# Two buffers of one-hots made a step ahead, a choice paced by piece length, and 79 halves in scoring

## Chip, cores and metric

The kernel runs on one core of one Trainium2 chip. The metric is the device time of one execution in microseconds (us), lower is better. Engines are named as in the profile: PE is TensorE, DVE is VectorE, ACT is ScalarE, POOL is GpSimd, SP the engine that only issues transfers.

## What is computed

One layer over 256 tokens of width 2048, all in float32: a normalised input goes through a projection to 5 x 1024 columns, half of them through differential attention and half through a gMLP; then an output projection and a residual; then PEER, an expert layer with 128 x 128 experts; then a final norm. The PEER layer fills most of the time:

```
q = (xb @ w_q).reshape(T, PEER_HEADS, 2, PEER_HALF)
sc = jnp.einsum('thcd,hckd->thck', q, sub_keys)
s1, i1 = lax.top_k(sc[:, :, 0], PEER_TOPK)
s2, i2 = lax.top_k(sc[:, :, 1], PEER_TOPK)
cand = (s1[..., :, None] + s2[..., None, :]).reshape(T, PEER_HEADS, PEER_TOPK * PEER_TOPK)
best, ci = lax.top_k(cand, PEER_TOPK)
...
idx = e1 * PEER_N_KEYS + e2
g = jax.nn.softmax(best.astype(jnp.float32), axis=-1)
act = jax.nn.gelu(jnp.einsum('td,thkd->thk', xb, u_sel))
out = jnp.einsum('thk,thkd->td', g.astype(act.dtype) * act, v_sel)
```

Each token takes 8 heads x 16 = 128 of the 16384 experts.

## The kernel before

**Two ways for two sets of tokens.** For 200 of the 256 tokens (`ND`) the kernel does not gather: it multiplies them with the whole table of `u` (the scoring), applies gelu and a dense matrix of gates that is zero for the experts not taken, and multiplies with the whole table of `v`. For the other 56 tokens it gathers rows of the tables by indirect DMAs of POOL (`gather`), half a row (1024 elements) for each of 128 picks at a time, and DVE makes their dot products and weighted sums: the *halves*, 232 in all (`half_rows`, line 1245 or 1253), each about 1.2 us of DVE. `HALF_STEPS` says in which steps of the scoring one is done, `HALF_UNITS` in which units of the v products. A half waits for its gather; three buffers (`PICKED`) are in turn, and the gather of half k+3 waits for half k.

**Units and steps.** A table comes in units of 128 x 1024 (512 KB, queued by SP). Every unit is split into a high part (ACT, `top`, line 720) and a low part (DVE, `low`, line 1188; POOL in a few steps, `by_pool`, line 477). PE does eight products with the high part and the hi and lo of x side by side (400 columns, line 1634), and one unit later eight with the low part (200 columns, line 1640). A *step* j of the scoring is two units, 2j and 2j+1, and fills row j of `store`. There are 128 steps, then 256 units of v (lines 1674 and 1679).

**What each engine does in a step, in this order.** DVE: `sum_halves(j)` (line 1197: adds the two halves of the PSUM bank, one of them copied out by ACT as `HOLES`, line 745), the low parts of units 2j+4 and 2j+5, then whatever stands in this step beside them, then `land(j)` (line 1224) and the halves. ACT: `HOLES` of step j, the high parts of 2j+5 and 2j+6, the gelu, and what stands beside. PE is one to two steps ahead of DVE's number: the low part made in DVE's step j is multiplied in PE's step j+2.

**Beside the steps** stand, one after another: 

- the *choice* (`piece`, 58 pieces that are left after 24 early ones): top-16 of the scores and of the 256 candidates, then comparisons that turn places into expert numbers. `piece_steps` says how many pieces each step has; before, one in odd and two in even steps, from step 1 to 39. When the pieces of a step are plain (top-16 only), POOL makes one of its two low parts. Two steps after the last piece of each tile of tokens PE transposes the picks (`PICKS_AT`).
- the *spread* of the gates, 50 steps from `SPREAD0` (43 before), four tokens a step: DVE compares indices with 0..127 (`one_hots`, line 1206, into `ONE`), ACT scales one of the two by the gate (`gates_into`, line 766, four instructions), PE multiplies them into a 128 x 128 matrix of gates for each token (`spread`, line 1618, after PE's step), DVE multiplies the rows of `store` that are done (`apply_gates`, line 1216), and ACT copies the gates of the rows to come (`put_gates`, line 757). `ONE` is one buffer, so `one_hots(b)` waits for `spread(b-1)`.
- after the spread, more halves: three in two steps up to step 120.

Before the scoring the queries are made from 32 units, whose low parts DVE and POOL share (`QUERY_BESIDE`, line 464). Early in it POOL also multiplies the 56 gathered tokens by a gain (line 458). The second group of these tokens (`X8`, five loads of 24 rows of 8 KB) was loaded by POOL when the scoring ended.

Of the kernel before, what the change touches and what calls it, by code (L numbers as in the profile page):

```python
# [11 lines left out]
ACT = mybir.ActivationFunctionType  # L12
# [63 lines left out]
QUERY_BESIDE = range(WQ0 + 9, WQ_END, 2)  # L76
CHOICE0 = 1


def piece_steps():  # L80

    steps, j = [], CHOICE0
    rest = 2 * (PIECES - EARLY)
    while len(steps) < rest:
        steps += [j] * min(2 - j % 2, rest - len(steps))
        j += 1
    return [-1] * EARLY + steps[:PIECES - EARLY] + [-1] * EARLY + steps[PIECES - EARLY:]
# [5 lines left out]
              for j in range(NKEYS)}  # L93
# [6 lines left out]
SPREAD0 = PICKS_AT[1] + 2  # L100
# [6 lines left out]
                    + list(range(SPREAD_END, NKEYS - 7, 2)))  # L107
# [14 lines left out]

SEL_A_AT = 2 * NKEYS - 4
# [26 lines left out]
def hybrid_peer_block(nc, x, w_in, w_out, wq_t, keys_t, u_t, peer_u, peer_v, ws_t, bs_t, gain_t, ffn_gain, z_gain,  # L150
                      final_gain, lambdas, rope, out):
    ctx = ExitStack()
    with ctx:  # L153
# [68 lines left out]
        ONE = at("ONE", 108 * KB, [P, 2, TOKB, NKEYS])  # L222
# [180 lines left out]
        def _(pool):  # L403
# [57 lines left out]
            for n in QUERY_BESIDE:  # L461
                pool.wait_ge(hi_ready, n + 1)
                pool.wait_ge(used, n - (LO_SLOTS - 1))
                nc.gpsimd.tensor_tensor(LO[:, n % 2, :], RAW[:, n % 4, :], HI[:, n % 4, :].bitcast(FP32),
                                        ALU.subtract).then_inc(lo_ready[n % 2], 1)
                if n == WQ0 + 9:
                    keys(2)
                if n == WQ0 + 17:
                    keys(3)
                if n - WQ0 in (21, 23, 25, 27):  # L470
                    r = (n - WQ0 - 21) // 2
                    pool.wait_ge(xg_saved, 16)
                    pool.dma_start(X4[r * NA:(r + 1) * NA, :], xg_dram[0:NA, :]).then_inc(x4_ready, 16)
# [41 lines left out]
            for r in range(ROWS_B):  # L515
                pool.dma_start(X8[r * NB_:(r + 1) * NB_, :], xg_dram[NA:NS, :]).then_inc(x8_ready, 16)
# [4 lines left out]
            for k in range(len(HALF_STEPS) + ROW_SLOTS, HALVES):  # L521
                gather(k)
                if HALF_UNITS[k - ROW_SLOTS - len(HALF_STEPS)] >= NKEYS + 50 and late:
                    pool.wait_ge(low_used, N_U + NKEYS + 44)
                    dst, src, done = late.pop(0)
                    pool.dma_start(dst, src).then_inc(done, 16)
# [8 lines left out]
        def _(act):  # L535
# [225 lines left out]
            def gates_into(b):  # L761

                act.wait_ge(compared, b + 1)
                for i in range(TOKB):
                    t = b * TOKB + i
                    ins = nc.scalar.activation(ONE[:, 1, i, :], ONE[:, 1, i, :], ACT.Copy, scale=EG[:, 2, t:t + 1])  # L766
                ins.then_inc(ones, 1)
# [18 lines left out]
            for j in range(NKEYS):  # L786
# [11 lines left out]
                if 0 <= j + 1 - SPREAD0 < N_BATCH:  # L798
                    gates_into(j + 1 - SPREAD0)
# [4 lines left out]
                if j in PICKS_AT:  # L804
                    picks_to_rows(PICKS_AT.index(j))
                if j == FIRST_WEIGHTS_AT:
                    weights_hi(0)
# [44 lines left out]
        def _(dve):  # L852
# [347 lines left out]
            def one_hots(b):  # L1200
# [3 lines left out]
                dve.wait_ge(g_done, b)  # L1204
                t0 = b * TOKB
                v.tensor_tensor(ONE[:], IOTA[:].unsqueeze(1).unsqueeze(1).broadcast_to([P, 2, TOKB, NKEYS]),  # L1206
# [63 lines left out]
            for j in range(NKEYS):  # L1270
# [11 lines left out]
                if 0 <= b + 1 < N_BATCH:  # L1282
                    assert done == [PIECES, PIECES]
                    one_hots(b + 1)
                if 0 <= b < N_BATCH:
                    apply_gates(b)
                if b >= 0:
                    land(j)
# [69 lines left out]
        def _(pe):  # L1358
# [253 lines left out]
            def spread(b):  # L1612
# [4 lines left out]
                for t in range(TOKB):  # L1617
                    last = mm(PS[:, G_BANK + b % 2, t * NKEYS:(t + 1) * NKEYS], ONE[:, 0, t, :], ONE[:, 1, t, :],
# [164 lines left out]
```

## Time and profile before

| | |
|---|---|
| three runs | 1829.03 us median (1823.68 to 1829.89) |
| profiled execution | 1811.19 us, span 1809.4 us, 28831 instructions |
| TensorE clock granted | 0.994 of full over the span |
| PE busy | 1731.2 us, 96% |
| DVE, ACT, POOL busy | 1439.8, 983.7, 478.0 us |
| DMA | 483.79 MB, 267 GB/s in the mean |

The profiled execution is 1% shorter than the three runs. PE's busy time is near the span; what is left is read stage by stage from windows and from the timeline. An idle time in brackets names what ended it.

### The profile page before, as it was taken

The page shows a single profiled execution, that of the slowest core. Times are in us where ns is not written, and L with a number is a line of the kernel's source. Part 1 is how long each engine was busy: PE and PEld are TensorE (multiplying, and loading weights), DVE is VectorE, ACT ScalarE, POOL GpSimd, SP SyncE. Part 2 cuts the span into 40 slices and gives each one's busy share as a digit, 9 for nine tenths or more (in the row PEclk, how much of TensorE's full clock was granted, in tenths as well). Part 3 has the DMA queues.
Part 4 walks back from the last instruction along what each step waited for, and adds up shares of the span by engine and source line. Part 5 has one row for each costly group of instructions (what it writes and reads, how often), then busy time and mean ns, then how long its engine had stood idle before and what let it go on. Part 6 is the DMA issues. An engine that isn't in the chain of part 4 may idle for free. (4 is left out here: it accounts for less than half of the span.)

```text
span 1809.4 us, 28831 instructions
## 1 busy us (share of the span) xinstructions
PE 1731.2 (96%) x10934; PEld 1638.0 (91%) x10934; DVE 1439.8 (80%) x2020; ACT 983.7 (54%) x1600; POOL 478.0 (26%) x327
## 2 busy tenths in 40 slices
PE   8999999999999999889889999999999999999997
PEld 7887788788999999888888999999999999999997
DVE  4546786568799987777788888778889999888995
ACT  5445564443565556666666545555555555555553
POOL 0002300034222001221221445315444224343231
PEclk9999999999999999999999999999999999999998
DMA  7665455666677776666666999899999999999992
GB/s 235 211 186 163 144 159 175 208 223 205 205 225 227 238 242 219 219 221 213 221 215 215 332 348 357 295 309 344 360 348 365 372 358 350 373 377 401 367 375 97
DMA packets 132855, 483.79 MB, mean 267 GB/s; under 512 B 15368, under 2 KB 15522, under 8 KB 132048
## 3 DMA queue, kind: packets, MB, share of 16 engines
q1 hardware_dynamic: 95760, 347.65, 57.4%
q0 software_dynamic: 36672, 133.77, 19.6%
q8 instruction: 87, 1.43, 0.3%
q10 hardware_dynamic: 288, 0.55, 0.1%
q14 instruction: 48, 0.39, 0.1%
HBM read 476.71 MB, written 5.20 MB: 266 GB/s over the span
## 5 line engine op out<-in xcount | busy, mean ns | idle before, releaser
L1674 PE MATMUL PS<-W,HI 128*128 128x400 f32 x2048 | 425.0, 348 | 9.3 <-DVE W L1264 5.6
L1634 PE MATMUL PS<-xT,HI 128*128 128x400 f32 x2048 | 422.2, 348 | 1.6 <-ACT HI L720 1.6
L720 ACT ACTIVATE HI<-V_RAW 128x1024 fp32r<-128x1024 f32 x256 | 271.4, 1061 | 280.0 <-PE PS L1674 135.0
L1674 PEld LDWEIGHTS PS<-W,HI 128*128 128x128 f32 x2048 | 358.4, 189 | 12.7 <-ACT HI L720 6.9
L1634 PEld LDWEIGHTS PS<-xT,HI 128*128 128x128 f32 x2048 | 358.0, 190 | 1.9 <-ACT HI L720 1.7
L1181 DVE TENSOR_TENSOR V_LO<-V_RAW,HI 128x2048 fp32r<-128x2048 f32 x128 | 292.7, 2287 | 24.1 <-ACT HI L720 23.7
L486 POOL DMA_INDIRECT PICKED<-peer_u,PK x116 | 179.5, 1547 | 490.9 <-DVE DOTS L1245 480.8
L720 ACT ACTIVATE HI<-RING_RAW 128x1024 fp32r<-128x1024 f32 x256 | 268.9, 1050 | 46.0 <-DMA RING_RAW<-u_t 41.3
L1188 DVE TENSOR_TENSOR RING_LO<-RING_RAW,HI 128x1024 fp32r<-128x1024 f32 x246 | 289.5, 1217 | 1.6 <-ACT HI L720 1.6
L1640 PEld LDWEIGHTS PS<-xT,RING_LO 128*128 128x128 f32 x2048 | 265.2, 191 | 16.1 <-DVE RING_LO L1188 15.9
L1640 PE MATMUL PS<-xT,RING_LO 128*128 128x200 f32 x2048 | 267.2, 273 | 12.3 <-DVE RING_LO L1188 12.2
L1679 PEld LDWEIGHTS PS<-W,V_LO 128*128 128x128 f32 x2048 | 268.6, 191 | 0.9 <-DVE V_LO L1181 0.9
L1679 PE MATMUL PS<-W,V_LO 128*128 128x200 f32 x2048 | 267.8, 272 | 0.6 <-DVE V_LO L1181 0.6
L486 POOL DMA_INDIRECT PICKED<-peer_v,PK x116 | 178.2, 1537 | 273.5 <-DVE ACC L1253 248.1
L864 DVE TENSOR_TENSOR LO<-RAW,HI 128x1024 fp32r<-128x1024 f32 x120 | 147.7, 1233 | 126.7 <-PE PS L1386 96.1
L538 ACT ACTIVATE HI<-RAW 128x1024 fp32r<-128x1024 f32 x144 | 152.6, 1066 | 163.7 <-PE PS L1386 58.2
L1253 DVE SCALAR_TENSOR_TENSOR ACC<-PICKED,DOTS,ACC 128x1024 f32<-128x1024 f32 (+1 forms) x112 | 142.8, 1281 | 42.4 <-DMA PICKED<-peer_v,PK 41.8
L1245 DVE CUSTOM_DVE_ANT_0 PICKED<-PICKED,X 128x1024 f32<-128x1024 f32 (+1 forms) x116 | 140.7, 1220 | 17.9 <-DMA PICKED<-peer_u,PK 17.7
L1379 PE MATMUL PS<-HI,xT 128*128 128x512 f32 x440 | 139.5, 398 | 2.1 <-ACT xT L563 1.4
L1386 PE MATMUL PS<-HI,xT 128*128 128x512 f32 x440 | 136.1, 391 | 0.6 <-DVE xT L883 0.6
L766 ACT ACTIVATE ONE<-ONE,EG 128x128 f32<-128x128 f32 x200 | 63.9, 390 | 95.6 <-DVE ONE L1206 95.6
L1386 PEld LDWEIGHTS PS<-HI,xT 128*128 128x128 f32 x440 | 82.6, 188 | 18.4 <-DVE xT L883 1.0
(213 smaller groups left out, 1668.0 us busy)
## 6 DMA issues: line engine op xcount, KB each, us to landing
RING_RAW<-u_t SPq DMA_DIRECT2D x256, 512.0 KB, 4.5
V_RAW<-peer_v SPq DMA_DIRECT2D x256, 512.0 KB, 7.3
RAW<-w_in SPq DMA_DIRECT2D x80, 512.0 KB, 3.9
RAW<-w_out SPq DMA_DIRECT2D x32, 512.0 KB, 3.7
RAW<-wq_t SPq DMA_DIRECT2D x32, 512.0 KB, 4.7
x_spill<-X POOLq DMA_DIRECT2D x2, 1024.0 KB, 5.8
X1R<-x_spill POOLq DMA_DIRECT2D x8, 256.0 KB, 10.5
PICKED<-peer_u,PK POOLq DMA_INDIRECT x116, 7.8
```

The costliest lines, as they stand in the source:

```text
L486: pool.indirect_dma_start(PICKED[k % ROW_SLOTS][:], None, table.rearrange("e (a c) -> (e a) c", a=2), bass.IndirectOffsetOnAxis(PK4[:, hal ...
L538: nc.scalar.activation(HI[:, slot, :], RAW[:, slot, :], ACT.Copy).then_inc(hi_ready, 1)
L720: nc.scalar.activation(HI[:, n % HI_SLOTS, :], raw_of(n), ACT.Copy).then_inc(top_ready, 1)
L864: v.tensor_tensor(LO[:, u % 2, :], RAW[:, u % 4, :], HI[:, u % 4, :].bitcast(FP32), ALU.subtract).then_inc(lo_ready[u % 2], 1)
L1181: nc.vector.tensor_tensor(pair_of(V_LO, v), pair_of(V_RAW, v), HI[:, slot:slot + 2, :].bitcast(FP32), ALU.subtract)\
L1188: v.tensor_tensor(low_of(n), raw_of(n), HI[:, n % HI_SLOTS, :].bitcast(FP32), ALU.subtract).then_inc(low_dve, 1)
L1253: ins = v.scalar_tensor_tensor(acc, rows, DOTS[0:np_, 0, g:g + 1], acc, ALU.mult, ALU.add)
L1386: ins = mm(banks[c], low(tt), h[:, halves[c]], start=False, stop=last and tt > 0)
L1634: return mm(PS[:, j % S_BANKS, 0:2 * ND].rearrange("p (a t) -> p a t", a=2), HI[:, n % HI_SLOTS, kk * P:(kk + 1) * P], xT[:, k, :, 0:ND], ...
L1640: return mm(PS[:, j % S_BANKS, 0:ND], low_of(n)[:, kk * P:(kk + 1) * P], xT[:, k, 0, 0:ND], start=False, stop=k == KT - 1)
L1674: return mm(PS[:, V_BANKS[i], 0:2 * ND].rearrange("p (a t) -> p a t", a=2), HI[:, v % HI_SLOTS, i * P:(i + 1) * P], weights_of(v), start=v ...
L1679: return mm(PS[:, V_BANKS[i], 0:ND], low_of(N_U + v)[:, i * P:(i + 1) * P], weights_of(v)[:, 0, :], start=False, stop=v % NKEYS == NKEYS - 1)
```

## The change

It has five parts.

- `ONE` has two buffers. DVE makes `one_hots(b+2)` in the step in which it applies gates b, after the apply instead of before it (before: `one_hots(b+1)`, ahead of the apply), and waits for one product less. ACT scales them one step earlier too, after `put_gates` instead of before.
- `piece_steps` gives pieces by a length for each kind, 2.6 us (3.4 where the piece is plain) of room a step. The 58 pieces take steps 1 to 32 instead of 1 to 39; the spread runs from step 37 to 86 instead of 43 to 92. POOL makes 8 low parts instead of 10.
- After the spread every fourth step has a second half instead of every second one; since this part starts six steps sooner, 79 halves instead of 78 are in the scoring.
- In the query stage DVE makes the low part of unit `WQ0 + 9` instead of POOL, and the keys that POOL loaded after it go with unit `WQ0 + 11`.
- `X8` is loaded after gather 99, about unit 35 of the v products, instead of at the end of the scoring.

```diff
-QUERY_BESIDE = range(WQ0 + 9, WQ_END, 2)
+QUERY_BESIDE = range(WQ0 + 11, WQ_END, 2)
...
+def piece_cost(i):
+
+    if i < HC:
+        return 1.55
+    if HC + 2 <= i < HC + 2 + PH:
+        return 2.35
+    return 0.5 if i in (HC + 2 + PH, HC + 2 + PH + 7) else 1.4
...
-    rest = 2 * (PIECES - EARLY)
-    while len(steps) < rest:
-        steps += [j] * min(2 - j % 2, rest - len(steps))
+    left = [i for o in range(2) for i in range(EARLY, PIECES)]
+    while left:
+        room += 2.6
+        if left[0] in PLAIN and (len(left) < 2 or left[1] in PLAIN):
+            room += 0.8
+        while left and piece_cost(left[0]) <= room + 0.4:
+            room -= piece_cost(left.pop(0))
+            steps.append(j)
         j += 1
...
-SPREAD0 = PICKS_AT[1] + 2
+SPREAD0 = PICKS_AT[1] + 3
...
-                    + list(range(SPREAD_END, NKEYS - 7, 2)))
+                    + list(range(SPREAD_END, NKEYS - 7, 4)))
...
+X8_AT = len(HALF_STEPS) + 20
...
-        ONE = at("ONE", 108 * KB, [P, 2, TOKB, NKEYS])
+        ONE = at("ONE", 104 * KB, [P, 2, 2, TOKB, NKEYS])
...
-            for r in range(ROWS_B):
-                pool.dma_start(X8[r * NB_:(r + 1) * NB_, :], xg_dram[NA:NS, :]).then_inc(x8_ready, 16)
...
+                if k == X8_AT:
+                    for r in range(ROWS_B):
+                        pool.dma_start(X8[r * NB_:(r + 1) * NB_, :], xg_dram[NA:NS, :]).then_inc(x8_ready, 16)
...
-                if 0 <= j + 1 - SPREAD0 < N_BATCH:
-                    gates_into(j + 1 - SPREAD0)
                 if 0 <= j - SPREAD0 < N_BATCH:
                     put_gates(j - SPREAD0)
...
+                if 0 <= j + 2 - SPREAD0 < N_BATCH:
+                    gates_into(j + 2 - SPREAD0)
...
-                dve.wait_ge(g_done, b)
+                if b > 1:
+                    dve.wait_ge(g_done, b - 1)
...
-                if 0 <= b + 1 < N_BATCH:
-                    assert done == [PIECES, PIECES]
-                    one_hots(b + 1)
                 if 0 <= b < N_BATCH:
                     apply_gates(b)
+                if 0 <= b + 2 < N_BATCH:
+                    assert done == [PIECES, PIECES]
+                    one_hots(b + 2)
```

The order on DVE in a step of the spread that also has a half. `TMP<-PS,HOLES` is `sum_halves`, `RING_LO` the two low parts, `ONE` the one-hots, `store<-store,PS` the gates applied, `store<-store,TMP` is `land`, `ISA` the half. Before, step 62:

```order
L1197 TENSOR_TENSOR TMP<-PS,HOLES 128x200 [waits landed,copied,low_used]
L1188 TENSOR_TENSOR RING_LO<-RING_RAW,HI 128x1024 [waits top_ready] x2
L1206 TENSOR_TENSOR ONE<-IOTA,EG 128x1024 [waits g_done]
L1216 TENSOR_TENSOR store<-store,PS 128x62x4 [waits gelus,g_done]
L1224 TENSOR_TENSOR store<-store,TMP 128x80 [waits g_put,gelus]
L1245 ISA PICKED_100,DOTS<-PICKED_100,X_95 128x1024 [waits row_ready0]
```

With the change, the same step (its line numbers are about 17 higher):

```order
L1214 TENSOR_TENSOR TMP<-PS,HOLES 128x200 [waits landed,copied,low_used]
L1205 TENSOR_TENSOR RING_LO<-RING_RAW,HI 128x1024 [waits top_ready] x2
L1234 TENSOR_TENSOR store<-store,PS 128x62x4 [waits gelus,g_done]
L1224 TENSOR_TENSOR ONE<-IOTA,EG 128x1024 [waits g_done]
L1242 TENSOR_TENSOR store<-store,TMP 128x104 [waits g_put,gelus]
L1263 ISA PICKED_101,DOTS<-PICKED_101,X_95 128x1024 [waits row_ready1]
```

The gates are applied ahead of the one-hots, and these are the ones for the product after the next.

The order on ACT in a step of the spread, from one `HOLES` to the next. Before:

```order
L745 ACTIVATE HOLES<-PS 128x8x25 [waits summed,low_used]
L720 ACTIVATE HI<-RING_RAW 128x1024 [waits low_dve,top_used,ring_ready1]
L730 ACTIVATE store<-TMP 128x136 [waits summed]
L731 ACTIVATE TMP<-TMP 128x64
L720 ACTIVATE HI<-RING_RAW 128x1024 [waits low_dve,top_used,ring_ready2]
L766 ACTIVATE ONE<-ONE,EG 128x128 [waits compared]
L766 ACTIVATE ONE<-ONE,EG 128x128 x3
L757 ACTIVATE store<-PS 128x70x4 [waits g_mul]
L745 ACTIVATE HOLES<-PS 128x8x25 [waits summed,low_used]
```

With the change:

```order
L762 ACTIVATE HOLES<-PS 128x8x25 [waits summed,low_used]
L737 ACTIVATE HI<-RING_RAW 128x1024 [waits low_dve,top_used,ring_ready3]
L747 ACTIVATE store<-TMP 128x108 [waits summed]
L748 ACTIVATE TMP<-TMP 128x92
L737 ACTIVATE HI<-RING_RAW 128x1024 [waits low_dve,top_used,ring_ready4]
L774 ACTIVATE store<-PS 128x69x4 [waits g_mul]
L783 ACTIVATE ONE<-ONE,EG 128x128 [waits compared]
L783 ACTIVATE ONE<-ONE,EG 128x128 x3
L762 ACTIVATE HOLES<-PS 128x8x25 [waits summed,low_used]
```

The copy of the gates now stands ahead of the scaling, and between the scaling and the next `HOLES` nothing is left.

## Rows read from the trace of the kernel before

**Rows 1.** The page, busy time of each engine.

```profile
PE 1731.2 (96%) x10934; PEld 1638.0 (91%) x10934; DVE 1439.8 (80%) x2020; ACT 983.7 (54%) x1600; POOL 478.0 (26%) x327
```

**Rows 2.** Windows: choice, spread, steps after it; us, busy by engine, PEclk, DMA share, GB/s.

```profile
469.00:675.60 206.60, 203.34 (x1385) 202.16 (x1384) 188.30 (x365) 120.03 (x181) 35.24 (x25) 1.00 0.71 229
675.60:997.30 321.70, 290.98 (x2002) 282.56 (x2002) 252.37 (x365) 204.19 (x499) 64.05 (x33) 1.00 0.66 219
997.30:1166.80 169.50, 158.88 (x1059) 155.96 (x1058) 146.52 (x210) 85.49 (x136) 73.60 (x44) 0.99 0.93 339
```

**Rows 3.** Timeline of PE at stage bounds: start, us, engine, line, operation.

```profile
656.47 1.64 PE L1634 MATMUL PS<-xT,HI 128*128 128x400 f32 x8
...
675.55 1.64 PE L1634 MATMUL PS<-xT,HI 128*128 128x400 f32 x8
...
997.27 1.64 PE L1634 MATMUL PS<-xT,HI 128*128 128x400 f32 x8
...
1162.09 1.63 PE L1634 MATMUL PS<-xT,HI 128*128 128x400 f32 x8
```

**Rows 4.** Timeline of PE in one step of the spread.

```profile
774.47 1.16 PE L1618 MATMUL PS<-ONE 128*128 128x128 f32 x8 [0.91 <-ACT ONE L766]
...
776.92 1.04 PE L1640 MATMUL PS<-xT,RING_LO 128*128 128x200 f32 x8
777.79 1.64 PE L1634 MATMUL PS<-xT,HI 128*128 128x400 f32 x8
779.27 1.03 PE L1640 MATMUL PS<-xT,RING_LO 128*128 128x200 f32 x8
```

**Rows 5.** Timeline of DVE and ACT around the same step.

```profile
771.89 1.22 DVE L1206 TENSOR_TENSOR ONE<-IOTA,EG 128x1024 f32<-128x1024 f32 x1
773.03 0.38 DVE L1216 TENSOR_TENSOR store<-store,PS 128x228 f32<-128x228 f32 x1
773.14 1.28 ACT L766 ACTIVATE ONE<-ONE,EG 128x128 f32<-128x128 f32 x4 [1.98 <-DVE ONE L1206]
...
774.61 0.33 ACT L745 ACTIVATE HOLES<-PS 128x200 f32<-128x200 f32 x1
774.81 0.22 DVE L1224 TENSOR_TENSOR store<-store,TMP 128x60 f32<-128x60 f32 x1 [1.40 <-ACT store L757]
...
775.16 0.37 DVE L1197 TENSOR_TENSOR TMP<-PS,HOLES 128x200 f32<-128x200 f32 x1
...
777.72 1.22 DVE L1206 TENSOR_TENSOR ONE<-IOTA,EG 128x1024 f32<-128x1024 f32 x1
```

**Rows 6.** Choice: timeline, and DVE's L1197 group in steps 1 to 39.

```profile
474.35 0.37 DVE L1197 TENSOR_TENSOR store<-PS,HOLES 128x200 f32<-128x200 f32 x1 [2.06 <-ACT HOLES L745]
...
615.47 1.14 PE L1640 MATMUL PS<-xT,RING_LO 128*128 128x200 f32 x8 [2.34 <-DVE RING_LO L1188]
...
661.81 0.37 DVE L1197 TENSOR_TENSOR store<-PS,HOLES 128x200 f32<-128x200 f32 x1 [0.91 <-ACT HOLES L745]
...
L1197 DVE TENSOR_TENSOR store<-PS,HOLES 128x200 f32<-128x200 f32 x39 | 14.3, 367 | 9.5 <-ACT HOLES L745 8.4
```

**Rows 7.** DMA issues after the spread: count, KB, median us to landing.

```profile
PICKED<-peer_u,PK POOLq DMA_INDIRECT x26, 8.5
```

**Rows 8.** Timeline of the query stage, units WQ0+8 to WQ0+10.

```profile
384.26 4.77 POOL L458 TENSOR_TENSOR X<-X,FGAIN 56x1024 f32<-56x1024 f32 x2 [4.78 <-DMA X<-xs_spill]
386.33 1.12 PE L1415 MATMUL PS<-xT,LO 128*128 128x256 f32 x8
387.79 2.33 DVE L864 TENSOR_TENSOR LO<-RAW,HI 128x1024 fp32r<-128x1024 f32 x1 [0.35 <-PE PS L1405]
392.38 2.08 PE L1415 MATMUL PS<-xT,LO 128*128 128x256 f32 x8 [3.08 <-POOL LO L464]
```

**Rows 9.** Timeline where the v products begin.

```profile
1171.93 2.59 POOL L516 DMA_DIRECT2D X<-xg_spill  x5 [21.04 <-DVE TMP L1197]
...
1188.09 2.24 ACT L720 ACTIVATE HI<-V_RAW 128x1024 fp32r<-128x1024 f32 x2 [4.72 <-DMA V_RAW<-peer_v]
```

More of the change, by code:

```diff
@@ L75 @@
 EARLY = 12
-QUERY_BESIDE = range(WQ0 + 9, WQ_END, 2)
+QUERY_BESIDE = range(WQ0 + 11, WQ_END, 2)
 CHOICE0 = 1
-def piece_steps():
-    steps, j = [], CHOICE0
-    rest = 2 * (PIECES - EARLY)
-    while len(steps) < rest:
-        steps += [j] * min(2 - j % 2, rest - len(steps))
+def piece_cost(i):
[4 more added lines that the diff above has]
+    return 0.5 if i in (HC + 2 + PH, HC + 2 + PH + 7) else 1.4
+def piece_steps():
+    steps, j, room = [], CHOICE0, 0.0
+    left = [i for o in range(2) for i in range(EARLY, PIECES)]
[6 more added lines that the diff above has]
+            steps.append(j)
         j += 1
-    return [-1] * EARLY + steps[:PIECES - EARLY] + [-1] * EARLY + steps[PIECES - EARLY:]
+    n = PIECES - EARLY
+    return [-1] * EARLY + steps[:n] + [-1] * EARLY + steps[n:]
 PIECE_STEPS = piece_steps()
@@ L465, in _ @@
                                         ALU.subtract).then_inc(lo_ready[n % 2], 1)
-                if n == WQ0 + 9:
+                if n == WQ0 + 11:
                     keys(2)
@@ L765, in gates_into @@
                     t = b * TOKB + i
-                    ins = nc.scalar.activation(ONE[:, 1, i, :], ONE[:, 1, i, :], ACT.Copy, scale=EG[:, 2, t:t + 1])
+                    ins = nc.scalar.activation(ONE[:, b % 2, 1, i, :], ONE[:, b % 2, 1, i, :], ACT.Copy, scale=EG[:, 2, t:t + 1])
                 ins.then_inc(ones, 1)
@@ L1203, in one_hots @@
                     dve.wait_ge(picks_out, TT)
-                dve.wait_ge(g_done, b)
+                if b > 1:
+                    dve.wait_ge(g_done, b - 1)
                 t0 = b * TOKB
-                v.tensor_tensor(ONE[:], IOTA[:].unsqueeze(1).unsqueeze(1).broadcast_to([P, 2, TOKB, NKEYS]),
+                v.tensor_tensor(ONE[:, b % 2], IOTA[:].unsqueeze(1).unsqueeze(1).broadcast_to([P, 2, TOKB, NKEYS]),
                                 EG[:, 0:2, t0:t0 + TOKB].unsqueeze(3).broadcast_to([P, 2, TOKB, NKEYS]), ALU.is_equal)\
@@ L1617, in spread @@
                 for t in range(TOKB):
-                    last = mm(PS[:, G_BANK + b % 2, t * NKEYS:(t + 1) * NKEYS], ONE[:, 0, t, :], ONE[:, 1, t, :],
+                    last = mm(PS[:, G_BANK + b % 2, t * NKEYS:(t + 1) * NKEYS], ONE[:, b % 2, 0, t, :], ONE[:, b % 2, 1, t, :],
                               start=True, stop=True)
```

## Prediction

> **What bounds the kernel now.** I read the page first: PE is busy 96% of the span, no other engine over 80% [rows 1]. So only what lets PE wait, or gives it fewer products, moves the end; the change leaves the products as they are. Next the windows, one for each stage. In the choice PE is nearly full. In the spread it is busy 291 of 321.7 us while DVE and ACT are far from full: a chain of waits, not a lack of time. In the steps after it PE is busy 159 of 169.5 us and the DMA share is 0.93 [rows 2]. Then the timeline of PE, for its pace where nothing holds it: low products 0.87 us from start to start (776.92 to 777.79), high products 1.48 (777.79 to 779.27), so 2.35 us a unit and 4.69 us a step [rows 4]. Against that pace:
>
> - spread: from 675.55 to 997.27 stand 50 steps, 6.43 us each [rows 3]. Undisturbed it would be the four fp32 products and the two units: 774.47 to 779.27 plus the 0.87 of the last low products, 5.67 us [rows 4]. PE loses 38 us here.
> - after the spread: 32 steps between 997.27 and 1162.09 take 164.8 us instead of 150.1: 14.7 us lost [rows 3].
>
> **Spread: the one-hots a step ahead.** What holds PE is its wait of 0.91 us for ACT's scaled one-hots [rows 4]. ACT in turn had waited 1.98 us for DVE's comparison, and DVE then waits 1.40 us, until ACT has copied the gates, before it can land the step [rows 5]. In steps with a half DVE starts the next step only behind that half, which makes them 6.7 us. With the change PE's one-hots are a full step old when it wants them, so this wait goes. What is late next is the ring DVE-ACT-DVE, since `HOLES` stands behind the scaling on ACT. I add it up from [rows 5]: `sum_halves` to the end of the low parts 2.56 (775.16 to 777.72); the gates applied, 0.38 shown, about 0.30 until the next instruction starts (as 1.22 shown is 1.14 from start to start); comparison to scaling 1.25 (771.89 to 773.14); scaling to `HOLES` 1.47 in the row, less about 0.28 for the copy that stood between, 1.19; `HOLES` to the next sum 0.43 (0.33 for itself and 0.1 of signal; the row's 0.55 holds a land too). Sum 5.73 us. The gates applied get longer with the rows of `store`, which makes it about 5.65 to 5.85. A half no longer adds: DVE needs 2.56 + 0.30 + 1.14 + about 0.2 for the land + 1.14 = 5.34. The land's wait is over before its turn, since the copy needs only the apply. So ring and PE (5.67) are nearly even; I take 5.77 us. 50 x 5.77 = 288.5 against 321.7, and 1 us for the entry: **-32 us** (bounds -36 at PE's own pace, -18 if a step takes 6.05).
>
> **Choice: the same pieces in 32 steps.** From 474.35 to 661.81 DVE does steps 1 to 39 in 187.46 us and waits 9.5 of it [rows 6]; so the work is 178.0. Seven steps fewer take away 7 x 2.56 of sums and low parts, two low parts that POOL no longer makes add 2 x 1.14: 162.4 us for 32 steps. My adding up of single pieces gives up to 2 more, so 163. PE wants 32 x 4.69 = 150.1. DVE is 13 us too long: it becomes the bound here. How much PE does not feel: an unhurried DVE starts its step 5.34 after PE's products of unit 2j+1 (661.81 against 656.47 [rows 3, 6]), and PE asks for that step's low part two steps of 4.69 later, which leaves 9.38 - 5.34, about 4 us. So PE stands still for 9 us, in pieces of up to 2.6 (two top-16 of 256 candidates in one step), as it does once now for 2.34 [rows 6]. Then comes what is queued behind: PE transposes the picks two steps after the last piece as before, but DVE arrives there 3.6 us late and with one piece more in its last step, where it used to be 2.6 us early: 3.6 + 1.3 - 2.6, some 2 us more. 11 us lost where now 4.4 are (from the starts of PE's steps, of which [rows 6] shows the longest wait): **+7 us** (bounds +2, if more lag is hidden, to +14).
>
> **After the spread: five halves in four steps.** A gather lands 8.5 us after its issue [rows 7]; with the wait for the freed buffer and the half itself (0.4 + 1.2) one of three buffers turns in 10 to 10.5 us, a half every 3.4 us. Three halves in two steps ask for one every 3.13 us: these steps are bound by the gathers, which holds up DVE and through its low parts PE. Five in four steps ask for one every 3.75 us. DVE's own work is 2.56 + 0.27 + 1.25 x 1.14 = 4.26 us a step. The DMA engines get 2 x 0.52 MB a step for `u` and 1.25 x 0.52 for halves, 363 GB/s instead of the 390 now asked for; they moved 339 [rows 2], so they will be nearly full, and I leave 3 us of the 14.7: **-11.5 us** (bounds -14.7 and -3). The halves left for the v products are 153 instead of 154: nothing. Six more steps stand after the spread and as many fewer before it: nothing for PE.
>
> **Query stage.** PE stands 3.08 us for POOL's low part, and the eight products behind it take 2.08 instead of 1.12 us: 4.0 us [rows 8]. POOL was late because of its multiplication by the gain, 384.26 to 389.03. DVE is free at about 386.75, within that multiplication. Its low part that started at 387.79 took 2.33 instead of 1.22 us and so ended 1.1 us after POOL was done [rows 8]. Read as a wait for POOL, the new one would run from 389.03 to 390.2, 1.1 us after PE wants it (386.33 + 2.8); read as half speed it would end at 389.1, in time. I take the first: **-3 us** (bounds -4 and -1). The Trainium skill ("SBUF — State Buffer", section on the two separate sides) says that the port pair which VectorE with two inputs and GpSimd share is an exclusive lock, not a split of bandwidth; by it the wait of 1.1 us comes, by a split it would not, and the row's 2.33 fits a lock from 387.79 to 389.03.
>
> **X8 elsewhere.** Its five loads, 0.98 MB, are issued at 1171.93, just when PE's first v units are due, and ACT waits 4.72 us for one of them [rows 9]. Out of the way they free 2.6 to 4 us of DMA time there. At unit 35 they ask for as much, in a stretch where the DMA engines are nearly full, but with units loaded ahead. **-1.5 us** (bounds -5 and +3).
>
> **Sum.** -32 + 7 - 11.5 - 3 - 1.5 = -41 us on the profiled execution's 1811.2: 1770. The three runs lie 1% above the profiled execution; I scale with them, 1770 x 1829.0 / 1811.2 = **1788 us**.
>
> **Rivals.**
> - *The ring holds at 6.1 us or more*: for it speaks that it runs at 5.8 to 5.85 already in steps without a half, with a margin of only 0.1 us to PE; against it, that nothing in the sum is unseen. -41 + 16 = -25, 1804 us. Chance 0.12.
> - *The steps after the spread stay bound by transfers*: the DMA share is 0.93 now, and the demand falls by 7% only. Against it: DVE's waits there are on the gathers' turn. -41 + 8.5 = -32.5, 1796 us. Chance 0.12.
> - *The choice costs 20 us*: each stop of PE could be followed by slow products, as after the 3.08 us stop (0.96 us more for eight [rows 8]); against it, the eight after the stop of 2.34 took 1.14 against 1.04 [rows 4, 6]. -28, 1801 us. Chance 0.08.
> - *Slower*: ACT now stands at the scaling until DVE's last but one instruction, and `HOLES` and the next high part are queued behind it. If ACT's high parts then come too late for PE, the step is longer than now. The other parts give 9 us, so it decides when a step of the spread reaches 6.6 us for no change and 6.8 for slower by 0.5%. At 7.0 us: +29 - 9 = +20, 1849 us. Against it: in the ring above ACT has the next high part some 4 us before PE wants it. Chance 0.03.
> - *The one-hots don't matter at all*, since PE then waits for the apply through the PSUM banks: the spread stays at 6.43 and -9 is left, 1820 us. Chance 0.03; two banks are in turn as before.
>
> **How the numbers follow.** My forecast has 0.62: 1776 to 1798 by itself. The first three rivals reach 1804. Below, all terms at their good ends would give some -56, 1772 after scaling, and the profiled execution's own 1% would lie there too. 1772 to 1806 leaves about 2 in 10 out. About 0.5% (9 us) is what a measurement of this kernel can tell from no change. Faster by more: all but the last two rivals, 0.94. Within: half of what the last rival and mishaps between hold, 0.03. Slower: 0.03.
>
> **What would show it.** A step of the spread at 5.7 to 5.85 us on PE, with no wait for ACT at the products of the one-hots, and DVE waiting for `HOLES`. In the choice, waits of PE for `RING_LO` of some 9 us in all from DVE's steps 16 to 29 and one of 2 us at the transposes. After the spread nearly no wait for `PICKED`. In the query stage a wait of 1 us, now for DVE. It is wrong if the spread is over 6 us a step, or if the choice loses over 20 us.

## The result

The changed kernel takes 1784.33 us (median of 4, 1784.10 to 1785.27) against 1828.95 us before (median of 4): a ratio of 0.9763, 95% interval 0.9744 to 0.9782. The forecast was 1788, in a range of 1772 to 1806. Its profiled execution is as long as its other runs, 1784.2 us, span 1782.4. That of before had been 18 us under its runs, so the two traces shown here differ by 27 us only, where my sum had said 41. Both are taken up below.

### The profile page after: what moved, and what is told of

Read it like the earlier page. It is cut to its first block and busy times, and to the rows that moved or that the text cites. A ratio compares the mean times of both kernels' runs of the same rounds, so it can differ in the third digit from the quotient of the medians.

```text
span 1782.4 us, 28846 instructions
## 1 busy us (share of the span) xinstructions
PE 1726.1 (97%) x10934; PEld 1639.2 (92%) x10934; DVE 1443.7 (81%) x2029; ACT 987.6 (55%) x1600; POOL 425.3 (24%) x324
## 5 line engine op out<-in xcount | busy, mean ns | idle before, releaser
L1692 PE MATMUL PS<-W,HI 128*128 128x400 f32 x2048 | 429.3, 351 | 25.1 <-DVE W L1282 21.5
L1692 PEld LDWEIGHTS PS<-W,HI 128*128 128x128 f32 x2048 | 362.4, 191 | 28.5 <-issue 22.6
L502 POOL DMA_INDIRECT PICKED<-peer_u,PK x116 | 144.1, 1243 | 531.5 <-DVE DOTS L1263 518.8
L502 POOL DMA_INDIRECT PICKED<-peer_v,PK x116 | 167.0, 1439 | 324.0 <-DVE ACC L1271 240.8
L1404 PEld LDWEIGHTS PS<-HI,xT 128*128 128x128 f32 x440 | 82.5, 188 | 18.4 <-DVE xT L900 1.0
L1397 PEld LDWEIGHTS PS<-HI,xT 128*128 128x128 f32 x440 | 79.7, 188 | 17.2 <-ACT xT L580 1.5
```

What stands on the lines that cost most here:

```text
L502: pool.indirect_dma_start(PICKED[k % ROW_SLOTS][:], None, table.rearrange("e (a c) -> (e a) c", a=2), bass.IndirectOffsetOnAxis(PK4[:, hal ...
L1397: mm(banks[c], high(tt), h[:, halves[c]], start=first, stop=False)
L1404: ins = mm(banks[c], low(tt), h[:, halves[c]], start=False, stop=last and tt > 0)
L1692: return mm(PS[:, V_BANKS[i], 0:2 * ND].rearrange("p (a t) -> p a t", a=2), HI[:, v % HI_SLOTS, i * P:(i + 1) * P], weights_of(v), start=v ...
```

## The profile after

Line numbers of the changed kernel are up to 18 higher. The windows over the same three stages, choice, spread and the steps after it, at their own bounds (us, busy by engine, PEclk, DMA share, GB/s), which answer to [rows 2]:

```profile
464.90:652.10 187.20, 178.28 (x1192) 175.31 (x1192) 177.29 (x351) 103.02 (x161) 30.66 (x23) 0.99 0.69 219
652.10:935.30 283.20, 283.20 (x2002) 280.49 (x2002) 247.69 (x363) 205.84 (x494) 31.47 (x33) 1.00 0.77 248
935.30:1119.70 184.40, 183.81 (x1250) 182.97 (x1250) 164.99 (x235) 104.24 (x160) 81.65 (x45) 1.00 0.95 349
```

In the spread PE is now busy all the time, as it is after it; in the choice it is not, and DVE is busy 95%. The timeline of PE at the stage bounds, as [rows 3], and at its waits in the choice, as [rows 6] (L1643 transposes the picks):

```profile
548.97 0.55 PE L1643 MATMUL PS<-IDENT,ROWS 128*128 128x128 f32 x3 [1.72 <-DVE ROWS L1158]
...
579.79 1.14 PE L1658 MATMUL PS<-xT,RING_LO 128*128 128x200 f32 x8 [2.35 <-DVE RING_LO L1205]
580.77 1.64 PE L1652 MATMUL PS<-xT,HI 128*128 128x400 f32 x8
...
592.00 1.33 PE L1658 MATMUL PS<-xT,RING_LO 128*128 128x200 f32 x8 [2.34 <-DVE RING_LO L1205]
593.12 2.92 PE L1652 MATMUL PS<-xT,HI 128*128 128x400 f32 x8
...
635.34 0.55 PE L1643 MATMUL PS<-IDENT,ROWS 128*128 128x128 f32 x3 [1.49 <-DVE ROWS L1158]
...
652.13 1.64 PE L1652 MATMUL PS<-xT,HI 128*128 128x400 f32 x8
...
935.33 1.63 PE L1652 MATMUL PS<-xT,HI 128*128 128x400 f32 x8
...
1115.02 1.64 PE L1652 MATMUL PS<-xT,HI 128*128 128x400 f32 x8
```

The waits for `RING_LO` in the choice are four with 5.5 us in all, those at the transposes two with 3.2. Behind the first long one the products keep their pace (1.64 at 580.77); behind the second, 12 us later, eight take 2.92 instead of 1.64 us, and the granted clock has fallen:

```profile
594.00:597.00 3.00, 3.00 (x16) 2.98 (x15) 2.90 (x7) 1.24 (x2) 0.00 (x0) 0.63 0.45 175
```

50 steps of the spread take 283.2 us (652.13 to 935.33), 5.66 each instead of 6.43. The 38 steps after it take 179.7, where 38 x 4.692 is 178.3: 1.4 us lost instead of 14.7.

One step in the middle of the spread on all three engines, as [rows 4, 5]:

```profile
784.55 0.37 DVE L1214 TENSOR_TENSOR TMP<-PS,HOLES 128x200 f32<-128x200 f32 x1 [0.32 <-issue]
...
786.21 1.64 PE L1652 MATMUL PS<-xT,HI 128*128 128x400 f32 x8
787.10 0.40 DVE L1234 TENSOR_TENSOR store<-store,PS 128x240 f32<-128x240 f32 x1
787.42 1.22 DVE L1224 TENSOR_TENSOR ONE<-IOTA,EG 128x1024 f32<-128x1024 f32 x1
...
788.55 1.07 PE L1636 MATMUL PS<-ONE 128*128 128x128 f32 x8
788.67 1.28 ACT L783 ACTIVATE ONE<-ONE,EG 128x128 f32<-128x128 f32 x4 [0.74 <-DVE ONE L1224]
789.38 1.70 PE L1652 MATMUL PS<-xT,HI 128*128 128x400 f32 x8
789.86 0.32 ACT L762 ACTIVATE HOLES<-PS 128x200 f32<-128x200 f32 x1
...
790.27 0.37 DVE L1214 TENSOR_TENSOR TMP<-PS,HOLES 128x200 f32<-128x200 f32 x1 [1.47 <-ACT HOLES L762]
```

PE takes the one-hots without a wait at 788.55; ACT only begins to scale the next ones at 788.67. The ring is there as foreseen: the times from each start to the next, from one `sum_halves` (784.55) over the low parts, the apply, the comparison, ACT's scaling and `HOLES` to the next `sum_halves` (790.27), are 2.55 + 0.32 + 1.25 + 1.19 + 0.41 = 5.72 us, and DVE now waits for `HOLES`.

The v products: after their first row they took 639.4 us before and take 659.5 now. One place stands out, right behind the loads of X8:

```profile
1225.35 2.58 POOL L539 DMA_DIRECT2D X<-xg_spill  x5
...
1246.88 1.28 DVE L1271 SCALAR_TENSOR_TENSOR ACC<-PICKED,DOTS,ACC 128x1024 f32<-128x1024 f32 x1 [10.82 <-DMA PICKED<-peer_v,PK]
...
1248.80 3.00 PE L1692 MATMUL PS<-W,HI 128*128 128x400 f32 x8 [11.23 <-DVE W L1282]
1251.61 1.86 PE L1697 MATMUL PS<-W,V_LO 128*128 128x200 f32 x8
```

DVE waits 10.8 us for a gather, and the weights of the v products that it makes are queued behind that half, so PE waits 11.2 us. Then its granted clock is 0.50, the lower of its two levels (1.2 GHz), and the next groups take 3.00 and 1.86 instead of 1.64 and 1.04 us. Windows there:

```profile
1230.00:1245.00 15.00, 7.58 (x53) 7.40 (x52) 3.75 (x3) 4.84 (x6) 3.96 (x2) 0.88 1.02 235
1245.00:1255.00 10.00, 6.20 (x22) 6.18 (x23) 8.12 (x7) 1.60 (x2) 5.40 (x2) 0.50 0.72 268
```

The DMA engines are fully busy for the 15 us of the first window but move 235 GB/s.

## The experiments

Each set of four ran on a chip of its own, beside runs of the kernel before: 1824.2, 1822.0 and 1807.8 us in the median for the three sets. So ratios are compared across sets, not times. That a ratio carries over from one chip to another is not shown: on the third chip even the kernel before is 14 us shorter, and no profile of it was taken there. Kernels of one set can be compared by their times. `a_` starts from the changed kernel, `b_` from the one before. Times by stage are read from each profile as above: what the choice loses against 4.692 us a step, the 50 steps of the spread, what the steps after it lose, and the time from the first v product to the end of the span. Each row is one profile.

| kernel | choice lost | spread | after it lost | halves in v | v products | ratio to before |
|---|---|---|---|---|---|---|
| before | 4.8 | 321.7 | 14.7 | 154 | 639.4 | |
| before, again | 5.1 | 321.6 | 12.2 | 154 | 649.1 | 0.9997 |
| changed | 13.6 | 283.2 | 1.4 | 153 | 659.5 | 0.9763 |
| a_x8_old | 13.5 | 284.2 | 2.0 | 153 | 651.8 | 0.9741 |
| a_x8_thin | 13.6 | 284.1 | 2.7 | 153 | 648.4 | 0.9741 |
| a_x8_apart | 13.6 | 283.8 | 1.6 | 153 | 655.3 | 0.9764 |
| a_x8_scoring | 13.5 | 284.5 | 4.1 | 153 | 647.4 | 0.9772 |
| b_onehots | 7.7 | 286.6 | 8.5 | 156 | 660.8 | 0.9823 |
| b_pace | 13.4 | 321.1 | 13.1 | 144 | 641.5 | 1.0018 |
| b_halves | 4.8 | 321.2 | 1.6 | 161 | 659.6 | 1.0029 |
| a_oldpace | 4.8 | 284.6 | 0.1 | 163 | 659.9 | 0.9862 |
| a_ring | 13.5 | 279.3 | 6.4 | 153 | 643.8 | 0.9763 |
| a_dense | 13.5 | 283.8 | 5.6 | 136 | 630.7 | 0.9746 |
| a_dense_ring | 13.6 | 279.3 | 1.8 | 136 | 631.3 | 0.9713 |

### What the loads of X8 cost, and why

**a_x8_old**: the loads back at the end of the scoring.

```diff
             pool.wait_ge(summed, NKEYS)
+            for r in range(ROWS_B):
+                pool.dma_start(X8[r * NB_:(r + 1) * NB_, :], xg_dram[NA:NS, :]).then_inc(x8_ready, 16)
...
-                if k == X8_AT:
-                    for r in range(ROWS_B):
-                        pool.dma_start(X8[r * NB_:(r + 1) * NB_, :], xg_dram[NA:NS, :]).then_inc(x8_ready, 16)
```

> The changed kernel with one part undone: the five loads of X8 are issued by POOL at the end of the scoring, as before the change. Its profile lost 11.2 us in one wait (1248.80) some 12 us after these loads were issued in the middle of the v products, and about 3 us more of slow products behind it. Theory (bytes): while these loads run the DMA engines are busy but move 200 to 250 GB/s instead of 360, so the gathers and the v units are late; at the old place they cost the 4.4 us that the kernel before lost at the start of the v products. So 14 - 4 = 10 us less: 1774 us. Rival (issue): POOL's 2.6 us of issuing push the next gather out; the same result here. Third (chance): the long wait was an accident of that stretch and comes back elsewhere: 1784 us.

Measured 1777.13 us (1772.53 to 1777.82), ratio 0.9741 (0.9711 to 0.9770). The long wait is gone, and PE's longest wait in the v products is 2.2 us; they are 7.7 us shorter. That is less than the 10 us expected, and the interval of the ratio overlaps that of the changed kernel.

**a_x8_thin**: the same five instructions at the new place, with 128 of 2048 columns each. The dot products of the second group read the sums of the first instead of X8 (and wait for them), so the kernel leaves out the real values of these dot products.

```diff
-                        pool.dma_start(X8[r * NB_:(r + 1) * NB_, :], xg_dram[NA:NS, :]).then_inc(x8_ready, 16)
+                        pool.dma_start(X8[r * NB_:(r + 1) * NB_, 0:P], xg_dram[NA:NS, 0:P]).then_inc(x8_ready, 16)
...
+                        dve.wait_ge(halves, A_SUMS)
-                    x_rows = X4 if g < GROUPS_A else X8
+                    x_rows = ACC4 if g >= GROUPS_A else X4
```

> The changed kernel with the five loads of X8 at their new place, but only the first 128 of 2048 columns of each (12 KB instead of 192 KB); the dot products of the second group read the sums of the first group instead of X8, so their values are not the reference's, and their time is the same. Theory (bytes): the wait of 11 us in the v products goes, 1784 - 14 = 1770 us. Rival (issue): the same five instructions on POOL's queue, so the wait stays, 1780 to 1784 us.

Measured 1775.70 us (1772.73 to 1777.79), ratio 0.9741 (0.9711 to 0.9771). The window of this kernel at the same place:

```profile
1230.00:1245.00 15.00, 15.00 (x105) 14.99 (x105) 12.25 (x9) 8.55 (x10) 9.75 (x4) 1.00 1.00 357
```

With the five issues on POOL's queue but without their bytes PE is never idle and the DMA engines move 357 GB/s at the same share. So it is the bytes, not the issuing. By the ratios this kernel is 4 us faster than the changed one and not 14 as the theory said: PE has seven waits of 1.0 to 3.7 us at other places of the v products, 13.6 us in all.

**a_x8_apart**: the loads five gathers apart.

```diff
-                if k == X8_AT:
-                    for r in range(ROWS_B):
-                        pool.dma_start(X8[r * NB_:(r + 1) * NB_, :], xg_dram[NA:NS, :]).then_inc(x8_ready, 16)
+                r, rest = divmod(k - X8_AT, 5)
+                if 0 <= r < ROWS_B and not rest:
+                    pool.dma_start(X8[r * NB_:(r + 1) * NB_, :], xg_dram[NA:NS, :]).then_inc(x8_ready, 16)
```

> The changed kernel with the five loads of X8 each behind another gather, five gathers (about 18 us) apart, from gather 99 on. Theory (bytes): each load takes 3 us or so of the DMA engines' time, which the units loaded ahead and the three gather buffers take up; most of the 14 us goes: 1770 to 1776 us. If the engines' time is what counts in sum, since the v products are bound by transfers all along, the loss is only spread: 1780 to 1784 us.

Measured 1781.16 us (1777.07 to 1781.55), ratio 0.9764 (0.9735 to 0.9793). No long wait, but six of 0.7 to 2.0 us in that stretch. I had expected 1770 to 1776 of my own theory; its second branch (1780 to 1784) came. In its own set this kernel is 4.0 us slower than a_x8_old and 5.5 slower than a_x8_thin, so spreading the loads out does not take their cost away.

**a_x8_scoring**: the loads in steps 91 to 115 of the scoring.

```diff
+                r, rest = divmod(j - SPREAD_END - 4, 6)
+                if 0 <= r < ROWS_B and not rest:
+                    pool.wait_ge(g_done, N_BATCH)
+                    pool.dma_start(X8[r * NB_:(r + 1) * NB_, :], xg_dram[NA:NS, :]).then_inc(x8_ready, 16)
...
-                if k == X8_AT:
-                    for r in range(ROWS_B):
-                        pool.dma_start(X8[r * NB_:(r + 1) * NB_, :], xg_dram[NA:NS, :]).then_inc(x8_ready, 16)
```

> The changed kernel with the five loads of X8 in the scoring after the spread, six steps apart (steps 91, 97, 103, 109, 115), when the one-hots no longer need their place. PE lost only 1.4 us in these 38 steps. Theory (bytes, and room there): neither the start nor the middle of the v products is hit, and each load is taken up by units loaded ahead: 1768 to 1774 us. Rival: the DMA engines are as full there as in the v products, so the steps after the spread lose about what is won: 1778 to 1784 us.

Measured 1778.16 us (1775.43 to 1787.52), ratio 0.9772 (0.9734 to 0.9810). The v products are the shortest of the four (647.4), the steps before them lose 2.7 us more than in the changed kernel, and the median is not better than that of a_x8_old. The two can't be told apart; my theory (1768 to 1774) did not come.

### Each part alone

**before_again**: the kernel before, once more.

> The kernel before, unchanged, for a second profile: its first profiled execution was 18 us under its other runs, and its v products took 639 us where five profiles of kernels with the same or fewer gathers there took 647 to 660. Theory: all stages up to the v products repeat within 1 us (spread 321.7, steps after it 14.7 lost), and only the v products, which are bound by transfers, vary; span 1818 to 1827, v products 648 to 657. Rival: the difference lies in the profile itself, then the span is 1809 again.

Measured 1819.05 us (1817.22 to 1827.46), ratio 0.9997 (0.9977 to 1.0016), span 1817.7. The spread repeats to 0.1 us and the steps after it lose 12.2 instead of 14.7, more of a difference than the 1 us that I expected; the v products take 649.1 instead of 639.4 us:

```profile
1168.70:1815.00 646.30, 622.51 (x4193) 617.29 (x4191) 549.69 (x501) 334.95 (x415) 210.90 (x170) 0.99 0.94 337
```

So the first profiled execution of before was short in its v products and nowhere else: its first v product had even come 1.4 us later (1170.02 against 1168.60). Against this second profile the changed kernel's is 35 us shorter (1817.7 to 1782.4), 46 gained up to the first v product and 10 lost behind it.

**b_onehots**: the two buffers and the order around them, in the kernel before. Pacing, the rule for the halves, query stage and X8 stay as they were. Two places of the edit are shown; the waits and ACT's order change as in the full diff above.

```diff
-        ONE = at("ONE", 108 * KB, [P, 2, TOKB, NKEYS])
+        ONE = at("ONE", 104 * KB, [P, 2, 2, TOKB, NKEYS])
...
-                if 0 <= b + 1 < N_BATCH:
-                    assert done == [PIECES, PIECES]
-                    one_hots(b + 1)
                 if 0 <= b < N_BATCH:
                     apply_gates(b)
+                if 0 <= b + 2 < N_BATCH:
+                    assert done == [PIECES, PIECES]
+                    one_hots(b + 2)
```

> The kernel before with the one-hots alone: two buffers, made a step ahead, spread from step 44 on (76 halves in the scoring, two more in the v products). Theory: the spread takes 283 us instead of 321.7, all else stays, the two halves cost up to 3: 36 to 38 us less than before on the same chip. Rival (the new pacing and the smaller number of halves are needed too, since DVE would else be late at the spread's entry): under 30 us.

Measured 1790.19 us (1785.35 to 1796.81), ratio 0.9823 (0.9795 to 0.9851): 32 us less, between the 36 to 38 of the theory and the rival's 30. The spread takes 286.6 us, so this part alone gives 35 of the 38.5 there. PE's steps are 5.59 us long only up to the twelfth and, but for one of 6.13, 5.7 to 5.85 after it, where the changed kernel keeps 5.59 for 29 steps. At the entry 2.9 us more are lost than before. The v products have two halves more, and took 660.8 us in this profile, which was the longest of the four executions (1796.81).

**b_pace**: the new `piece_steps` alone.

```diff
-        steps += [j] * min(2 - j % 2, rest - len(steps))
+        while left and piece_cost(left[0]) <= room + 0.4:
+            room -= piece_cost(left.pop(0))
+            steps.append(j)
```

> The kernel before with the new piece_steps alone: the choice takes 32 steps, the spread starts at step 36, and 88 halves are in the scoring, 10 fewer in the v products. Theory: the choice costs 9 us more (13.6 lost instead of 4.4), eight more steps with three halves in two cost 3 to 4 more, and ten gathers fewer give back up to 1.4 us each in the v products, if transfers bound them: -2 to +5 us. Rival: the v products don't care for ten gathers: +13 us.

Measured 1822.31 us (1819.67 to 1830.43), ratio 1.0018 (0.9997 to 1.0039). The choice loses 13.4 us instead of 5, and the v products, with ten halves fewer, take 641.5 us, 7.6 less than in the second profile of before but 2.1 more than in the first. In the medians the two cancel, as expected. The 3 to 4 us more after the spread did not come (13.1 lost, as before).

**b_halves**: five halves in four steps alone.

```diff
-                    + list(range(SPREAD_END, NKEYS - 7, 2)))
+                    + list(range(SPREAD_END, NKEYS - 7, 4)))
```

> The kernel before with five halves in four steps after the spread alone, instead of six; 71 halves in the scoring and 7 more in the v products. Theory (gathers bound the steps after the spread): their loss falls from 14.7 to about 2 us. The seven halves come back in the v products at up to 1.4 us each, if these are bound by transfers: -3 to -6 us in all. Rival: the v products take them for nothing: -13 us.

Measured 1827.36 us (1817.79 to 1834.42), ratio 1.0029 (1.0007 to 1.0051). I had expected 3 to 6 us less and it is no faster, rather 0.1 to 0.5% slower. The loss after the spread is 1.6 us instead of 12 to 15, as the theory of the gathers says, and none of it is left in the end: seven halves more stand in the v products, which take 10.5 us more than in the second profile of before, although this was the shortest of the ten executions (1817.79):

```profile
1156.50:1813.00 656.50, 625.80 (x4193) 620.19 (x4191) 558.91 (x508) 335.34 (x415) 225.57 (x177) 0.98 0.94 337
```

The rate is the same, 337 GB/s at a DMA share of 0.94, as in the window above: more bytes, and so much more time. Seven gathers of 0.52 MB are 10.9 us at that rate.

**a_oldpace**: the changed kernel with the old `piece_steps`.

> The changed kernel with the old piece_steps: choice in steps 1 to 39, spread from step 44, 69 halves in the scoring and 163 instead of 153 in the v products. Theory (the pacing costs time in the choice and is paid back in halves): the choice loses 4.5 to 5 us instead of 13.6, and ten gathers more in the v products cost about 1 us each: 1783 to 1788 us, no difference that can be told. Rival (the new pacing is a plain loss): 1775 us.

Measured 1777.06 us (1772.85 to 1791.70), ratio 0.9862 (0.9809 to 0.9915), where a_ring in the same set has 0.9763. In its profile 8.8 us come back in the choice, and the v products with 163 halves take 659.9 us, where a_ring, with 153 of them, takes 643.8 on this chip. I had expected no difference against the changed kernel; the ratio is 1% over its 0.9763, and the two intervals don't meet. But that is across chips, and the changed kernel itself was not run on this one. Against a_ring, on the same chip, it is 12.5 us slower in the median and 6.2 in the profiles, and 5.3 us of that are the spread, which a_ring shortens by its own edit. Its four times lie 19 us apart. So whether the new pacing gains anything with the short spread stays open; in b_pace it gained nothing.

### What sets the spread now, and a better version

**a_ring**: ACT scales the one-hots behind the next `HOLES`.

```diff
                 low_half_out(j)
+                if 0 <= j + 1 - SPREAD0 < N_BATCH:
+                    gates_into(j + 1 - SPREAD0)
...
-                if 0 <= j + 2 - SPREAD0 < N_BATCH:
-                    gates_into(j + 2 - SPREAD0)
```

> The changed kernel with ACT's scaling of the one-hots moved behind HOLES of the next step, so that DVE's next sum no longer waits for it. Theory: in the later 20 of the 50 spread steps the ring DVE-ACT-DVE (5.68 to 5.82 us) is longer than PE's own 5.585; without it all steps take 5.59, the spread 279.5 instead of 283.2 us; in all 3 to 4 us less, near what can be told. Rival: something else lengthens these steps, PE or the apply on DVE, then the spread stays at 283.

Measured 1764.52 us (1760.59 to 1769.01), ratio 0.9763 (0.9737 to 0.9789). The spread takes 279.3 us, 5.587 a step from the first to the last. Its timeline in one step:

```profile
785.75 0.35 ACT L762 ACTIVATE HOLES<-PS 128x200 f32<-128x200 f32 x1 [1.13 <-PE PS L1658]
785.99 1.27 ACT L783 ACTIVATE ONE<-ONE,EG 128x128 f32<-128x128 f32 x4
786.19 0.37 DVE L1214 TENSOR_TENSOR TMP<-PS,HOLES 128x200 f32<-128x200 f32 x1 [0.69 <-ACT HOLES L762]
```

`HOLES` now waits for PE and for nothing else. So the ring it was, and PE's own pace is 5.59 us. The 4 us are not to be seen in the ratio; the steps after the spread lose 6.4 us in this profile instead of 1.4. They are seen where the edit stands alone between two kernels of one set, a_dense and a_dense_ring below.

This kernel still has its X8 loads in the v products, and its longest loss there is 10.2 us, at the same place: it was no accident of one execution. The rate of the DMA engines behind the loads falls to 247 GB/s (1225 to 1240). In a_oldpace, with the loads behind its gather 89, it falls to 266 (1205 to 1220), yet PE's longest wait is 3.4 us. So the lower rate comes back in all three kernels with the loads at one go, and the long wait in two of them.

**a_dense**: a half in every step of the spread, X8 at its old place.

```diff
-HALF_STEPS = sorted([j for j in range(SPREAD0 - 3, SPREAD_END) if j % 3] + list(range(SPREAD_END, NKEYS - 7))
+HALF_STEPS = sorted([j for j in range(SPREAD0 - 3, SPREAD_END)] + list(range(SPREAD_END, NKEYS - 7))
```

> The changed kernel with X8 at its old place (measured 1777) and a half in every step of the spread instead of two in three: 96 halves in the scoring, 136 in the v products. Theory: DVE has 5.4 us of work in such a step and PE and ACT set 5.6 to 5.8, so the spread stays at 284 us; 17 gathers fewer in the v products give back about 1 us each: 1757 to 1765 us. Rival (DVE is the bound as soon as every step has a half): the spread takes 290 or more, 1765 to 1770 us.

Measured 1759.12 us (1758.74 to 1762.93), ratio 0.9746 (0.9720 to 0.9772). The spread stays at 283.8 us, so 17 halves went in without making it longer, as DVE's 5.4 us of work allow. With 136 halves the v products take 630.7 us, and PE has only one wait of over 0.6 us left there, 3.1 us at their entry, where a_x8_old has eight:

```profile
1127.00:1755.00 628.00, 615.88 (x4193) 613.27 (x4191) 531.79 (x483) 335.00 (x415) 184.13 (x152) 0.99 0.92 332
```

The time lies in the range that I expected (1757 to 1765), but that was worked out from a_x8_old on another chip, and the ratio is no better than that kernel's 0.9741. In its own set, against a_ring, it is 5 us faster, with X8 elsewhere and without a_ring's edit. So what the denser halves alone give is not isolated.

**a_dense_ring**: the two diffs above together.

> The kernel of a_dense with the scaling moved as in a_ring. Theory: both gains add up, the spread at 280 to 281 us, 1754 to 1762 us in all. Rival: with a half in each step DVE itself (5.4 to 5.6 us) is level with PE, and nothing is won on top of a_dense.

Measured 1752.87 us (1752.45 to 1756.76), ratio 0.9713 (0.9687 to 0.9739), the fastest of all: 0.5% under the changed kernel's ratio (the intervals don't meet, but the chips differ), and 12 us under a_ring on the same chip. The spread takes 279.3 us and the v products 631.3. Against a_dense only the place of the scaling differs, and it is 6.2 us less; the two sets of four times do not overlap. 4.5 us of it are the spread, as the theory said: nothing is hidden by DVE's own work.

## Why the prediction was right, and where not

- **Spread, -32 us: mechanism right, size 6.5 us too small.** Measured -38.5 (321.7 to 283.2), outside my bound of -36, which should have been -37 by its own numbers (321.7 - 50 x 5.67, less 1 for the entry). The ring was summed to 5.73 us and is 5.72 in the middle. But PE does not follow it at once: up to step 66 PE takes 5.59 us a step and DVE falls behind a little in each, within its lag of 4 us, the very lag that I had used for the choice and forgot here. Only then the steps take 5.7 to 5.8. PE's own pace is 5.59 and not 5.67, since the fp32 products cost 0.83 us from start to start (788.55 to 789.38) when nothing is late, and 0.92 after a wait. a_ring, and a_dense_ring against a_dense, show that the ring is the rest.
- **Choice, +7 us: right, 2 us too small.** Measured +8.8 (13.6 lost against 4.8). DVE's 32 steps take 164.9 us (starts at 470.30 and 635.20), where my sum over all gave 162.4, the one over single pieces up to 2 more, and I took 163. The long waits stand where foretold, 2.3 us at steps with two large pieces and 1.5 at the second transposes. But the waits for `RING_LO` are 5.5 us in all and not 9, and I had left out the wait of 1.7 at the first tile's transposes. The rest of the 13.6 is smaller stops and slower products behind the waits, 1.4 us of it at 593.12 alone.
- **After the spread, -11.5 us: right in its stage, but not a gain by itself.** Measured -13.3 against the first profile of before and -10.8 against the second, and b_halves has it alone. There it is given back in the v products. In the change it is kept, since the new pacing gives six more steps for halves and their number stays.
- **Query stage, -3 us: right, and better by 1 us.** The scoring's step 1 starts 4.05 us earlier than in the first profile of before, and starts at 464 to 466 us in all `a_` kernels and at 469 to 472 in all others. PE has no wait there at all. The timeline:

```profile
385.17 5.82 POOL L474 TENSOR_TENSOR X<-X,FGAIN 56x1024 f32<-56x1024 f32 x2 [4.94 <-DMA X<-xs_spill]
387.50 1.23 DVE L881 TENSOR_TENSOR LO<-RAW,HI 128x1024 fp32r<-128x1024 f32 x1
...
389.25 2.82 DVE L881 TENSOR_TENSOR LO<-RAW,HI 128x1024 fp32r<-128x1024 f32 x1
389.88 1.12 PE L1433 MATMUL PS<-xT,LO 128*128 128x256 f32 x8
```

  The new low part (387.50) took its usual 1.23 us: it came between POOL's two multiplications, and POOL's pair took 5.82 instead of 4.77 us [rows 8], 1.05 longer. The next low part, within the second multiplication, took 2.82 and ended 1.1 us after it. So it is a lock in both directions, and whoever comes first has it. That fits what the Trainium skill says ("SBUF — State Buffer", section on the two separate sides); my wait of 1.1 us did not come because DVE was first. That was luck: DVE began 0.04 us ahead of POOL's second multiplication (387.54). The second profile of before has the other order once more: a low part from 387.75 took 3.19 us and ended 1.1 us after POOL's pair (389.85).
- **X8, -1.5 us: wrong, and outside its bounds in the trace.** The step that failed is "with units loaded ahead". Units of v are loaded ahead, but the gathers have three buffers only, and DVE's next half, and behind it the weights, hang on them. The loss at the entry went (the first eight units of v lose 2.0 us instead of 6.1 against 2.35 us a unit) and one of 14 us came. Against a_x8_old the place costs 7.7 us by the profiles, which is less than two profiles of one kernel can differ in this stage. By the ratios, 0.9763 and 0.9741, it is 4 us, and the intervals overlap. My size of the loads was wrong too: I took 0.98 MB at the full rate, 2.6 to 4 us; the engines moved 235 instead of 357 GB/s for 15 us, which is 15 x (357 - 235) = 1.8 MB not moved, 5 us at 357 GB/s, X8's own bytes counted as moved. Each load goes to 24 partitions. The Trainium skill has a rule on it ("SBUF — State Buffer", section "Door 1: The DMA port swizzle"): the bandwidth of a transfer depends on how many of the 16 ports its partitions reach. The trace agrees with a slow transfer that keeps all engines busy; no run here varied the partitions, so the cause is argued and only the cost of the bytes is shown.
- **The scaling by 1%: wrong reason.** I took the profiled execution of before as typical but for a constant factor. Its second profile shows that it was short in the v products alone. My sum from the profile, 1770 us, is 14 us under what was measured: the terms up to the v products came out 7.6 us better than said (47.1 measured from 1170.02 to 1122.95, 39.5 summed), X8 9 us worse, and the v products another 12 longer than in that one profile. The scaling added 18 us and covered these 14. So the mechanisms of the first four terms were right, and that the median was met to 4 us is luck.
- **Rivals.** The ring at 6.1, the choice at 20 and the two last did not come; what the rival on the choice rests on, slow products behind a stop, came once (593.12). The low end of my range took all good ends as -56 us, and they add up to -57.7. The one on transfers named the wrong stage: the steps after the spread kept their gain, and the v products are what transfers bound.

## What to carry to other kernels

When work is moved between stages, ask what each stage is bound by before counting a gain: here a gather in the last stage cost 0.8 us in one pair of profiles (649.1 - 641.5 for ten) and 1.5 in another (659.6 - 649.1 for seven), so one taken out of the scoring's end is worth nothing if it goes there. A ring over two engines shows in the bound engine only after its lag is used up, so a ring 2% longer than the bound costs less than its length says: nothing for 29 steps in the changed kernel, and for 12 in b_onehots. A single profile of a stage that is bound by transfers is not its time: take a second one before scaling with it.

## What the runs showed that I had not expected

- The v products vary by 10 us between two profiles of the same kernel (639.4 and 649.1), while the spread repeats to 0.1 us. The profiles with 136 halves have 631 us, those with 144 have 641.5, those with 153 and 154 have 639 to 660, and those with 156, 161 and 163 have 660 to 661. So more halves make them longer, but the place of X8's loads, the chip and plain variation hide what one half costs.
- Five loads of 192 KB to 24 partitions each hold the rate of the DMA engines at 235 GB/s for 15 us, at a share of 1.02; with the same issues and 12 KB each it is 357.
- After an idle time of 11.2 us PE's granted clock is 0.50, and eight products of 400 columns take 3.00 us. A much shorter idle time can be followed by the same: behind the wait of 2.34 us at 592.00 in the choice eight such products took 2.92 us, while behind the one of 2.35 at 579.79 they took 1.64. What makes the difference is open.
- On another chip the kernel before took 1807.8 us instead of 1822 to 1829.
